# Group norm of the attention outputs: two of three head groups normed inside the last head steps

## The reference

```python
def rms_norm(x, g):
    xf = x.astype(jnp.float32)
    y = xf * lax.rsqrt(jnp.mean(xf * xf, axis=-1, keepdims=True) + RMS_EPS)
    return (y * g.astype(jnp.float32)).astype(x.dtype)

def hybrid_mixer(...):
    ...
    out_a = dilated_attention(heads(qa, N_HEADS_A), heads(ka, N_HEADS_A), heads(va, N_HEADS_A))
    out_b = mla_attention(c_q, c_kv, k_rope, g_q, g_kv, w_uq, w_ukv)
    out_c = neighbourhood_attention(heads(qc, N_HEADS_C), heads(kc, N_HEADS_C), heads(vc, N_HEADS_C), rpb)
    y = jnp.concatenate([rms_norm(flat(out_a), g_out_a),
                         rms_norm(flat(out_b), g_out_b),
                         rms_norm(flat(out_c), g_out_c)], axis=-1)
    return jnp.einsum('bsf,fd->bsd', y, w_o)
```

## Time and profile before

| what | us |
|---|---|
| median of 3 runs (2593.35 to 2599.23) | 2597.82 |
| the profiled execution | 2598.39 |
| its span | 2596.6 |
| TensorE busy | 2461.5 (95%) |
| VectorE busy | 647.1 (25%) |
| ScalarE busy | 508.2 (20%) |
| GpSimd busy | 116.2 (4%) |
| last head steps and tail of layer 0 | about 300 to 340 us from the start |
| last head steps and tail of layer 1 | about 1070 to 1105 us |

### The profile page before, as it was taken

One profiled execution on the slowest core, in us unless ns is written; L12 is line 12 of the kernel. 1 busy time (PEld: TensorE's weight loads), 2 busy tenths in 40 slices (PEclk: granted clock), 3 DMA queues, 4 the chain that ended last, 5 costly groups with the idle time before them and its releaser, 6 DMA issues.

```text
span 2596.6 us, 38576 instructions
## 1 busy us (share of the span) xinstructions
PE 2461.5 (95%) x16160; PEld 2152.9 (83%) x16161; DVE 647.1 (25%) x1382; ACT 508.2 (20%) x1032; POOL 116.2 (4%) x100
## 2 busy tenths in 40 slices
PE   8999998999999999898989999999989999999994
PEld 5658746888886577647989998999989999999994
DVE  2256534433643255522010000010000010100103
ACT  1145413222421245411001001011010010101102
POOL 2021100000001030101000000000000000000001
PEclk9999998999999999999999999999999999999997
DMA  8200254333130210235875656768767777787883
GB/s 256 81 27 22 80 194 127 98 98 111 66 113 31 81 40 8 91 136 199 309 291 203 241 209 227 284 259 301 295 251 263 263 267 292 289 307 296 303 305 115
DMA packets 203138, 482.32 MB, mean 186 GB/s; under 512 B 4833, under 2 KB 31600, under 8 KB 202592
## 3 DMA queue, kind: packets, MB, share of 16 engines
q1 hardware_dynamic: 192208, 429.36, 44.9%
q0 software_dynamic: 8304, 40.82, 5.0%
q10 hardware_dynamic: 2448, 9.44, 0.9%
HBM read 459.93 MB, written 35.39 MB: 191 GB/s over the span
## 4 chain that ended last, share of the span: by engine, by line
PE 79%; issue 2%; DVE 2%; ACT 1%; DMA 0%; POOL 0%; DVEq 0%; ACTq 0%; POOLq 0%
PE ps L908 34%; PE ps L923 17%; PE ps L807 10%; PE ps L644 6%; PE ps L818 4%; PE ps L652 3%; PE ps L759 2%; PE ps L637 1%; PE ps L892 1%; PE ps L864 1%; PE ps L876 1%; DVE x_rows L1580 0%; PE ps L739 0%; PE ps L740 0%; DMA attention_arena<-results_by_slot,gains 0%
## 5 line engine op out<-in xcount | busy, mean ns | idle before, releaser
L908 PE MATMUL ps<-hT,attention_arena 128*128 128x128 f32 (+4 forms) x4096 | 526.1, 287 | 33.0 <-issue 33.0
L908 PEld LDWEIGHTS ps<-hT,attention_arena 128*128 128x128 f32 x4096 | 511.2, 194 | 34.9 <-issue 34.9
L1569 DVE TENSOR_TENSOR attention_arena<-ps,attention_arena 128x256 f32<-128x256 f32 x224 | 95.1, 424 | 1217.0 <-ACT attention_arena L1180 1217.0
L908 PE MATMUL ps<-hT,weight_ring 128*128 128x128 f32 (+4 forms) x3072 | 388.6, 283 | 0.0
L908 PEld LDWEIGHTS ps<-hT,weight_ring 128*128 128x128 f32 x3072 | 376.8, 191 | 0.0
L1180 ACT ACTIVATE attention_arena<-ps 128x256 f32<-128x256 f32 x224 | 86.1, 384 | 1128.5 <-PE ps L908 1128.4
L923 PE MATMUL ps<-attention_arena 128*128 128x128 f32 (+4 forms) x2048 | 266.1, 283 | 0.0
L644 PE MATMUL ps<-weight_ring,hT 128*128 128x384 f32 (+3 forms) x768 | 259.8, 499 | 3.3 <-DVE hT L1206 1.7
L923 PEld LDWEIGHTS ps<-attention_arena 128*128 128x128 f32 x2048 | 254.1, 191 | 0.0
L644 PEld LDWEIGHTS ps<-weight_ring,hT 128*128 128x128 f32 x768 | 147.7, 194 | 106.9 <-issue 63.4
L807 PE MATMUL ps<-x_high,w_parts 128*128 128x512 f32 x704 | 224.0, 399 | 5.5 <-ACT x_high L1075 5.5
(11 more groups left out here) (185 smaller groups left out, 1810.4 us busy)
## 6 DMA issues: line engine op xcount, KB each, us to landing
attention_arena<-in_e_w_dram SPq DMA_DIRECT2D x96, 2048.0 KB, 12.1
weight_ring<-in_e_w_dram SPq DMA_DIRECT2D x72, 2048.0 KB, 12.2
weight_ring<-in_w_dram SPq DMA_DIRECT2D x22, 1024.0 KB, 7.0
weight_ring<-in_w_dram SPq DMA_DIRECT2D x4, 2816.0 KB, 9.7
results_by_slot<-attention_arena ACTq DMA_DIRECT2D x9, 1024.0 KB, 9.8
weight_ring<-in_w_o_dram SPq DMA_DIRECT2D x4, 2048.0 KB, 8.1
attention_arena<-rows_by_slot POOLq DMA_DIRECT2D x8, 1024.0 KB, 11.2
weight_ring<-in_w_in_dram SPq DMA_DIRECT2D x2, 3072.0 KB, 10.8
```

The costliest lines, as they stand in the source:

```text
L908: last = nc.tensor.matmul(ps[:, f % 2, m * UNIT:m * UNIT + n], w[:, k, i * P:(i + 1) * P], XT[:, k, 0:n], start=(k == 0), stop=(k == ND - 1))
L1569: tt(eh[:, f % EHS, :], ps[:, f % 2, UNIT:2 * UNIT], esil[:, f % 2, :], ALU.mult).then_inc(gu_free, 1)
```

## The change

The columns of `ssq`, `rms` and `rr` are renumbered, so that one group's four sums stand side by side (`NT * i + t` in place of `3 * t + i`). At g = 52, behind the squares of group B, ScalarE takes the roots of the eight sums of groups A and B. VectorE takes their reciprocals at g = 55 and scales one row tile of one group in each of the steps 55 to 62. Behind the last head only the four sums of group C are left: one root, one reciprocal instruction and one scaling per row tile.

```diff
-                    square(on[:, t, c0:c1], 3 * t + i)
+                    square(on[:, t, c0:c1], NT * i + t)
...
                     if g in (HA * NT + 4, (HA + HB) * NT + 4):
                         group(l, 0 if g < (HA + HB) * NT else 1)
+                        if g > (HA + HB) * NT:
+                            own_root(0, 2 * NT)
                 group(l, 2)
-                own_root(0, 3 * NT)
+                own_root(2 * NT, 3 * NT)
...
+            def group_scaled(i, t):
+
+                c0, c1 = GROUPS[i]
+                return nc.vector.scalar_tensor_tensor(out=on[:, t, c0:c1], in0=on[:, t, c0:c1],
+                                                      scalar=rr[:, NT * i + t:NT * i + t + 1],
+                                                      in1=g_out[:, c0:c1], op0=ALU.mult, op1=ALU.mult)
...
+                    first_scaled = STEPS - 2 * NT - 1
+                    if g == first_scaled:
+                        roots_in(0, 2 * NT)
+                    if 0 <= g - first_scaled < 2 * NT:
+                        group_scaled(*divmod(g - first_scaled, NT))
                 head_out(l, NH - 1)
                 dve.wait_ge(o_out, (l + 1) * NH)
-                roots_in(0, 3 * NT)
+                roots_in(2 * NT, 3 * NT)
                 for t in range(NT + 2):
                     if t < NT:
-                        for i, (c0, c1) in enumerate(GROUPS):
-                            last = nc.vector.scalar_tensor_tensor(out=on[:, t, c0:c1], in0=on[:, t, c0:c1],
-                                                                  scalar=rr[:, 3 * t + i:3 * t + i + 1],
-                                                                  in1=g_out[:, c0:c1], op0=ALU.mult, op1=ALU.mult)
-                        last.then_inc(y_ready, 1)
+                        group_scaled(2, t).then_inc(y_ready, 1)
```

## The result

The changed kernel takes 2602.44 us (median of 16 runs, 2599.77 to 2604.68), the kernel before 2596.41 in the same comparison (16 runs, 2592.56 to 2599.23). The ratio is 1.0024, with a 95% interval of 1.0017 to 1.0031: slower by 6.0 us, between 4.4 and 8.1. A comparison on another chip gave 1.0025 (1.0015 to 1.0035). The forecast was 2602.4, with a range of 2597.0 to 2607.0. Its 58% stood on "within 0.2%", its 40% on "slower". The result lies at that bound: the ratio is just across 0.2%, but its interval reaches down to 0.17%, and the median lies just inside the 2603.0 that the prediction named.

The account below looks back on a forecast made before the run. TensorE, busy 95% of the span, was taken as the bound. Tail -2.2, ScalarE's delay less the strip's wait +4.4, scalings 0, clock +2.4 gave +4.6 us: median 2602.4, range 2597.0 to 2607.0.

Parts of the forecast that it names:

- The tail's gain: Behind the last head, fewer scalings and reciprocals bring the first transpose 1.1 us sooner per layer, 2.2 in both.
- at no difference: Tail pause of TensorE, cut from 6.32 to 5.2 us, would still lower the clock; no change in time counted.
- ScalarE's delay: Two table loads and a root ahead of step 55's exponential make TensorE late by 2.96 us per layer.
- The rival of a costly switch back: Switch back into the running exponential costs a restart like another load in each layer: 2605.0 us in total; chance 0.12.
- The late strip: TensorE's later wait for the last strip of biases takes back 1.07 us in layer 0, 0.45 in layer 1.
- VectorE's scalings: Eight scalings and a reciprocal in the head steps just fit under TensorE's steps; taken at 0, bounds 0 to 0.5 per layer.
- 3.7 of 4 us: VectorE's busy time in the head steps with the scalings added, up from 2.51 us in the 4 from 312 to 316.
- The clock: Behind the new pause TensorE's clock falls with chance 0.7 at a price of 1.65 us: 1.2 per layer, 2.4 in both.

Follow-up runs that it names:

- ScalarE's part alone: Changed kernel with the mid-loop root and its two table loads kept, but all twelve VectorE scalings back in the tail; 2601.42 us, ratio 1.0025 to the kernel before.
- the versions without the delay: Changed kernel with roots of groups A and B on GpSimd, no added table loads: scalings partly doubled in steps 58 to 63, 2596.95 us; single in 56 to 63, 2593.81.
- the changed kernel with the tail's filler: Changed kernel plus five matmuls issued by TensorE in each layer's tail pause; 2596.44 us against 2596.18 for the kernel before, ratio 0.9997.

## Why the prediction was right, and where its terms were off

**What bounds the kernel.** Right: TensorE stands still in the tail for a chain that it waits for, and a delay on ScalarE ahead of step 55 reaches TensorE whole.

**The tail's gain, 1.1 us per layer.** The first transposition comes 1.12 us sooner (8.87 to 7.75 from step 63). I had taken the clock of the tail "at no difference", and for that step there was no ground. The comparison with ScalarE's part alone puts what enters the time at 0.5 to 0.6 per layer, since there the clock came back at the same instant for both. Against the traced execution of the kernel before, where it came back later, it is 1.2 per layer, and with the clock held up 1.5. That the second of these is near the forecast owes something to the instant at which the clock came back.

**ScalarE's delay, 2.96 per layer.** Measured from step 54 to 55: 3.03. Both loads are 1.28, with no restart behind the second: the exponential starts 0.02 after it. The rival of a costly switch back is gone, and with it what the Trainium skill, "ScalarE: Activation LUTs", section "What ACT_TABLE_LOAD costs", adds to each load as a drain of 1380 ns: neither direction of the switch shows it here.

**The late strip, 1.07 and 0.45 taken back.** Right: the time from the transposes of step 56 to those of step 60 fell from 8.28 to 7.30 in layer 0 and from 7.66 to 7.20 in layer 1, 0.98 and 0.46.

**VectorE's scalings, taken at 0.** Right for the changed kernel (steps 60 to 63: 4.54 and 4.56, no more than before), but for a reason that the prediction did not give in full. They seem to be free because TensorE has just been made late, so that the strip is no longer waited for. The reckoning "3.7 of 4 us" was near the edge, and in the versions without the delay such scalings cost 0.57 per layer, and doubled ones 1.5. This was not tested by itself, since those versions also moved the scalings by a step or more. That a scaling excludes GpSimd's addition was not in the prediction at all.

**The clock, 1.2 per layer.** The price was 1.44 where the prediction had 1.65. The chance was too low: of the eight pauses of 3.14 to 3.16 us in the traces of the changed kernel (twice), of ScalarE's part alone and of the changed kernel with the tail's filler, seven lowered the clock. What enters the time is less than the price, by the stretches 0.4 to 1.2 us per layer where it falls, since at the full clock TensorE runs into VectorE, GpSimd and the strip instead.

**The sum.** +4.6 was forecast and +6.0 measured (4.4 to 8.1); the stretches of the traces give +4.8 and +4.5. Term by term, steps 54 to 63 were to lose 4.4 + 2.4 = 6.8 and lost 7.2 and 7.1 in these traces; the tail was to gain 2.2 and gained 2.4 and 2.5. The sum thus came out of the mechanism and not of large errors that cancel, but if the tail's gain is the 1.1 of the other comparison, it was too large by 1.1, and some +6 in place of +4.8 would follow from that. That the median met the forecast within 0.1 us is chance, since it also rests on a level of before that moved from 2597.82 (3 runs) to 2596.41 (16 runs).

What stays open: the medians put the effect of the lower clock behind the new pause at zero, give or take two microseconds or more (2601.24 against 2601.32, and 0.22 against 0.26 above the kernel before), and the stretches at 0.4 to 1.2 per layer where it falls. The two do not contradict one another, but the size rests on single executions. Open as well is when the tail's lower clock usually ends in the kernel before, and with it which of the tail's two gains enters the median.

## What to carry to other kernels

Work taken from behind the last step and put inside the steps is free only where the engine that gets it has a lead at that very place. A pair of table loads around one root cost 3 us at step 52 and 0.6 and 2.0 us (in the two layers) six steps later, where that engine waited anyway; and a scaling that was hidden in one order was not in another. Look behind the steps too: what doubled scalings cost showed up partly behind the last step.

Where the bounding engine stands still in a pause and sets in again at the lower clock, a cut of the pause is worth only half of its length as long as the clock comes back at the same instant. A few matmuls that kept it at work there gave 2.6 and 4.3 us by the medians and 3.3 by the stretches, in two layers; the cut alone gave 1.1 or 2.4, by which trace it is compared with. Since that instant moved by up to 3.6 us between the traces of this case, a difference of a microsecond in such a stretch of two single traces proves nothing by itself.

Before an instruction moves to an idle stretch of VectorE, see what GpSimd does there: the scaling and the mask's addition, each with two inputs in SBUF, made one another wait in these traces.

## What the runs showed of the hardware that I had not expected

- A scaling of 384 columns on VectorE, 0.61 us alone, took 1.34 to 2.08 us in eight places of these traces where GpSimd's addition of 1.77 us had begun first, and in all eight it ended 0.41 to 0.43 us behind the addition's end. Where VectorE was first, GpSimd's addition took up to 2.18 us, the longer the more the two overlapped.
- A switch of ScalarE from the exponential's table to the root's and back costs the two loads of 1.28 us, with 0.01 to 0.02 us between neighbours.
- The same pause of 3.15 us lowered TensorE's clock seven times of eight. In the changed kernel with the tail's filler it read 0.53 in the window behind the pause in layer 0 and 1.00 in layer 1.
- With one scaling per tile in the tail, the stretch from there to the norm took 64.38 us in layer 0 and 66.42 in layer 1 with the clock held up. Where it fell, the lower clock lasted for 2.8 to 5.6 us behind the first transposes, and each of these microseconds made the stretch 0.42 to 0.46 us longer (twelve pauses, an estimate from the stretches and the windows).
